# A new order of gate products and cache work, with GpSimd's page work given to VectorE and ScalarE

## The reference, cut to what matters

```
h = rms_norm(x) ; z = h @ w_in                  # u (512) | q | k | v (1024 each) | two gates (1024 each)
gate_pool = sigmoid(z[gates 0:1024]) ; gate_attn = sigmoid(z[gates 1024:])
pool_out  = _pool_mixer(u) ; o = attention(q, k, v)       # samples: over 512 cached positions + their own
merged = gate_pool * (pool_out @ w_pool_proj) + gate_attn * (o @ w_attn_proj)
x = x + merged @ w_o ; x = x + relu(rms_norm(x) @ w_up)^2 @ w_down ; y = rms_norm(x)

s = einsum('bqhcd,bkhcd->bhcqk', q, k) * HEAD_DIM ** -0.5  # two maps c per head
p = softmax(s) ; a = p[:, :, 0] - lam * p[:, :, 1] ; out = einsum('bhqk,bkhe->bqhe', a, v)
```

## Time and profile before

| | us |
|---|---|
| three runs, median | 1803.35 |
| the profiled execution | 1804.24 |
| its span (first to last instruction) | 1802.4 |
| TensorE busy | 1725.0 |
| VectorE busy | 1057.7 |
| ScalarE busy | 632.8 |
| GpSimd busy | 247.4 |
| DMA | 139.13 MB, mean 77 GB/s |

### The profile page before, as it was taken

How to read it: one execution, slowest core, us unless ns; L and a number is a source line. 1 busy time by engine, 2 the same in 40 slices (tenths; PEclk the granted TensorE clock), 3 DMA queues, 4 the chain that set the end, 5 groups by cost and what they waited for, 6 DMA issues and landing times.

```text
span 1802.4 us, 29113 instructions
## 1 busy us (share of the span) xinstructions
PE 1725.0 (96%) x11756; PEld 1668.6 (93%) x11756; DVE 1057.7 (59%) x1725; ACT 632.8 (35%) x1289; POOL 247.4 (14%) x284
## 2 busy tenths in 40 slices
PE   7999999999978788999999999999999999999997
PEld 6889888988958788999999999999999999999997
DVE  5677777777765986774223448454636363636454
ACT  4355555555543211113112445232414141414232
POOL 3222221222210655340000000000000000000001
PEclk9999999999979899999999999999999999999999
DMA  6202220221122565663112321211111111202112
GB/s 192 63 10 62 71 59 13 72 60 32 52 65 81 202 225 175 195 200 98 47 47 71 94 59 48 71 32 63 48 47 48 48 47 48 69 26 71 35 49 95
DMA packets 136525, 139.13 MB, mean 77 GB/s; under 512 B 6720, under 2 KB 114176, under 8 KB 136383
## 3 DMA queue, kind: packets, MB, share of 16 engines
q1 hardware_dynamic: 135239, 133.07, 23.8%
q10 hardware_dynamic: 1152, 4.19, 0.6%
HBM read 120.29 MB, written 17.18 MB: 76 GB/s over the span
## 4 chain that ended last, share of the span: by engine, by line
PE 83%; DVE 6%; POOL 3%; DMA 2%; issue 2%; ACT 2%; SPq 1%; DVEq 0%; ACTq 0%
PE ps L1072 20%; PE ps L782 18%; PE ps L1010 18%; PE ps L692 15%; PE ps L716 3%; PE ps L749 3%; POOL kv_pages L2138 2%; PE ps L739 1%; DMA q_bc<-q_sample_scratch 1%; POOL kv_pages L2144 1%; DVE kv_pages L1796 1%; DMA kv_pages<-in_cache_v 1%; DVE w_lo L1467 1%; PE ps L720 1%; DMA w_raw<-in_w_in 1%
## 5 line engine op out<-in xcount | busy, mean ns | idle before, releaser
L1988 DVE TENSOR_TENSOR x<-ps,x 128x1032 f32<-128x1032 f32 x64 | 78.9, 1232 | 223.4 <-PE ps L1072 223.4
L692 PE MATMUL ps<-w_hi,h_hi 128*128 128x384 f32 x520 | 182.3, 351 | 5.9 <-DVE w_lo L1467 3.8
L692 PE MATMUL ps<-w_hi,h_lo 128*128 128x384 f32 x520 | 176.7, 340 | 0.0
L692 PE MATMUL ps<-w_lo,h_hi 128*128 128x384 f32 x520 | 176.1, 339 | 0.0
L1072 PE MATMUL ps<-ff_lo,m_hi 128*128 128x344 f32 x768 | 162.9, 321 | 0.0
L1072 PE MATMUL ps<-ff_hi,m_lo 128*128 128x344 f32 x768 | 162.4, 320 | 0.0
L1072 PE MATMUL ps<-ff_hi,m_hi 128*128 128x344 f32 x768 | 162.1, 319 | 0.0
L1072 PEld LDWEIGHTS ps<-ff_lo,m_hi 128*128 128x128 f32 x768 | 129.1, 188 | 0.0
L1072 PEld LDWEIGHTS ps<-ff_hi,m_hi 128*128 128x128 f32 x768 | 128.4, 188 | 0.0
L1072 PEld LDWEIGHTS ps<-ff_hi,m_lo 128*128 128x128 f32 x768 | 128.2, 188 | 0.0
L1135 ACT ACTIVATE prob<-ps,nbias 128x256 f32<-128x256 f32 (+7 forms) x128 | 94.9, 742 | 88.9 <-DVE nbias L1526 86.4
(11 more groups left out here) (273 smaller groups left out, 4131.5 us busy)
## 6 DMA issues: line engine op xcount, KB each, us to landing
w_raw<-in_w_in SPq DMA_DIRECT2D x44, 512.0 KB, 6.0
kv_pages<-in_cache_k SPq DMA_DIRECT2D x32, 512.0 KB, 5.0
kv_pages<-in_cache_v SPq DMA_DIRECT2D x32, 512.0 KB, 5.1
m_pair<-in_w_up SPq DMA_DIRECT2D x16, 1024.0 KB, 5.5
m_down<-in_w_down SPq DMA_DIRECT2D x16, 1024.0 KB, 5.0
out<-kv_st SPq DMA_DIRECT2D x16, 512.0 KB
x_in<-in_x_prompt SPq DMA_DIRECT2D x8, 512.0 KB, 5.1
attention_out_scratch<-oT_st ACTq DMA_DIRECT2D x8, 512.0 KB, 2.6
```

Of the source, the lines that this page charges most:

```text
L692: mm = pe.matmul(bank[0:n, 0:3 * P], a[:, kt, toks(t)], w[:, :, kt, :], start=(kt == 0 and m == 0), stop=(kt == KT - 1 and m == 2))
L1988: dve.tensor_tensor(x1_chunks[:, n], psum_set(n % 2), x1_chunks[:, n], ALU.add).then_inc(s_xadd, 1)
```

## The change: what it does

The two hand-written loops go away: `PART_A` now holds all tiles up to the last `ga`, and the eight `ap` tiles follow in a row. Gates 6 and 7 move to the front, between the u tiles, and write to `merged[6]` and `merged[7]` themselves, since `gate` is one tile; `ga` results go to a new `ga_sig` of eight tiles. `up`, `o_hi` and `mg_lo` get other places: `o_hi` lies where `h_lo` was, so each of its tiles waits until the last `ga` product has read that k-tile (`s_hread`).

VectorE multiplies all four key pages in one instruction. Of the value pages VectorE still weighs two, and ScalarE the other two, in 16 instructions of 128x128 with a scale column. GpSimd does no page work. The work on the value pages moves from beside gate and pool tiles 4 to 7 to the last three pool tiles and the `ga` tiles. SP's order is written from step numbers: `V_LOAD_AT` says ahead of which weight load the value pages go.

The diff, cut to its core:

```diff
-PART_A = [("u", 0), ("u", 1), ("grp", 0), ("u", 2), ("grp", 1), ("u", 3), ("grp", 2), ("gate", 0), ("grp", 3),
-          ("pool", 0), ("gate", 1), ("pool", 1), ("gate", 2), ("pool", 2),
-          ("gate", 3), ("pool", 3)]
-REDUCE_AT = (1, 3, 5, 7, 9, 10, 11, 13)
+PART_A = [("u", 0), ("u", 1), ("gate", 6), ("grp", 0), ("u", 2), ("gate", 7), ("grp", 1), ("u", 3), ("grp", 2),
+          ("gate", 0), ("grp", 3), ("pool", 0), ("gate", 1), ("pool", 1), ("gate", 2), ("pool", 2), ("gate", 3), ("pool", 3),
+          ("gate", 4), ("pool", 4), ("gate", 5), ("pool", 5), ("pool", 6), ("pool", 7)] + [("ga", n) for n in range(KT)]
+OWN_AT, SCORES_AT, SELECT_AT, TAIL_AT = 5, 20, 21, 10
+REDUCE_AT = (2, 6, 10, 12, 13, 15, 16, 18)
+VALUES_AT = (23, 24, 25, 26, 27, 27, 28, 29)
+V_LOAD_AT = REDUCE_AT[6:] + (23, 23, 24, 25, 26, 27)
...
 # SP
+            def load_values(b):
+                if b < 2:
+                    sp.wait_ge(s_kred, DEC - 1 + b)
+                else:
+                    sp.wait_ge(s_v, b - 1)
+                load_pages(b, b % 2, cache_v)
...
+            for l in range(4, len(tile_at) + KT):
+                freed = (tile_at + list(range(S_ATTN, S_OUT)))[l - 4]
+                for b in range(2, DEC):
+                    if before <= REDUCE_AT[b - 2] < freed:
+                        load_keys(b)
+                for b in range(DEC):
+                    if before <= V_LOAD_AT[b] < freed:
+                        load_values(b)
+                if before <= TAIL_AT < freed:
+                    store_tail()
+                if before <= SELECT_AT < freed:
+                    load_samples()
...
+                if l < len(tile_at):
+                    load_a(l)
+                else:
+                    load(l // 2, l % 2, w_attn, KT, l - len(tile_at))
+                before = freed
...
 # TensorE: value sums b after these k-tiles
+            beside = {("u", 1): {1: last_head_out, 3: state_transposes}, ("ga", 0): {5: values_of(1)},
+                      ("ga", 1): {5: values_of(2)}, ("ga", 2): {1: values_of(3)}, ("ga", 3): {1: values_of(4), 7: values_of(5)},
+                      ("ga", 4): {5: values_of(6)}, ("ga", 5): {5: values_of(7)},
+                      ("ga", 6): {0: sample_norms, 3: spread_norms}}
...
+                if s_ == VALUES_AT[0]:
+                    cached_values(0)
...
 # ScalarE
+            def weigh_half(b):
+
+                act.wait_ge(s_pg[b % 2], PG_K + 16 * PAGES * (b // 2 + 1))
+                for g in range(PAGES // 2, PAGES):
+                    for h in range(HEADS):
+                        part = kv_pg[:, b % 2, g, h * P:(h + 1) * P]
+                        done = act.activation(part, part, ACT.Copy, scale=a_all[:, g, b * HEADS + h:b * HEADS + h + 1])
+                done.then_inc(s_vp, 1)
...
+                elif kind == "ga":
+                    if n == KT - 1:
+                        attention_high()
+                    sigmoid(t, chunks(ga_sig[:, n]))
+                    next_high(t)
+                    if n == 0:
+                        weigh_half(3)
+                    elif n == 1:
+                        weigh_half(4)
+                        weigh_half(5)
+                    elif n == 2:
+                        weigh_half(6)
+                    elif n == 3:
+                        weigh_half(7)
...
+                    if n == KT - 2:
+                        weigh_half(1)
+                    elif n == KT - 1:
+                        weigh_half(2)
...
 # VectorE
-                dve.tensor_tensor(kv_pg[:, b % 2, PAGES - 1], kv_pg[:, b % 2, PAGES - 1], q_bc[b % 2][:],
-                                  ALU.mult).then_inc(s_prod2, 1)
+                dve.tensor_tensor(kv_pg[:, b % 2], kv_pg[:, b % 2], q_bc[b % 2][:].unsqueeze(1).to_broadcast([P, PAGES, D]),
+                                  ALU.mult).then_inc(s_prod, 1)
...
+                elif kind == "ga":
+                    if n == 0:
+                        weigh_values(3)
+                        sum_values(2)
+                    elif n == 1:
+                        sum_values(3)
+                        weigh_values(4)
+                    elif n == 2:
+                        weigh_values(5)
+                        sum_values(4)
+                    elif n == 3:
+                        sum_values(5)
+                        weigh_values(6)
+                    elif n == 4:
+                        weigh_values(7)
+                        sum_values(6)
+                        sum_values(7)
+                    elif n == KT - 3:
+                        sample_outputs()
+                    elif n == KT - 2:
+                        sample_rows()
+                    elif n == KT - 1:
+                        attention_low()
+                    next_low(t)
...
+                    if n == N_EARLY - 1:
+                        weigh_values(0)
+                        weigh_values(1)
+                    elif n == KT - 2:
+                        sum_values(0)
+                    elif n == KT - 1:
+                        sum_values(1)
+                        weigh_values(2)
...
 # GpSimd
-            for b in range(DEC):
-                pool.wait_ge(s_pg[b % 2], 80 * (b // 2) + 80)
-                for g in range(PAGES - 1):
-                    part = kv_pg[:, b % 2, g]
-                    pool.tensor_tensor(part, part, q_bc[b % 2][:], ALU.mult).then_inc(s_prod, 1)
-            pool.wait_ge(s_vout, 1)
-            for i in range(0, DEC // 2):
-                for slot in range(2):
-                    pool.wait_ge(s_pg[slot], PG_K + 16 * PAGES * (i + 1))
-                    for g in range(PAGES // 2, PAGES):
-                        pool.tensor_tensor(*weighing(2 * i + slot, slot, g, 1), ALU.mult).then_inc(s_vp, 1)
```

More of the change, by code:

```diff
@@ L586, in _ @@
             load_keys(1)
[L587 to L599, removed]
@@ L614, in _, with store_tail @@
[L614 to L623, removed]
+            def store_tail():
+                sp.wait_ge(s_tailc, 1)
+                sp.dma_start(new_pool_p[0, 0], tail_st[0:BUF]).then_inc(s_out, 16)
+                sp.dma_start(new_pool_s[0, :, BUF - 1], tail_st[BUF:BUF + DEC]).then_inc(s_out, 16)
@@ L910, in select_weights, with cached_values, last_rows_ready @@
                 pe.matmul(bank_o[:, 256:320], ones_a[:], sel[:], start=True, stop=True).then_inc(s_sela, 1)
-            def cached_values(i, slot):
-                pe.wait_ge(s_vs, VS * (2 * i + slot + 1))
+            def cached_values(b):
+                pe.wait_ge(s_vout, 2)
+                pe.wait_ge(s_vs, VS * (b + 1))
                 for h in range(HEADS):
-                    mm = pe.matmul(ps[:, 6, bass.ds((2 * i + slot) * HEADS + h, 1)], kv_pg[:, slot, 0, h * P:(h + 1) * P],
+                    mm = pe.matmul(ps[:, 6, b * HEADS + h:b * HEADS + h + 1], kv_pg[:, b % 2, 0, h * P:(h + 1) * P],
                                    ones[:, 0:1], start=True, stop=True)
                 mm.then_inc(s_v, 1)
[L920 to L940, removed]
-            for i in range(0, DEC // 2):
[L942 to L945, removed]
-            for i in range(DEC // 2, KT - N_A):
-                product(gate_tile(i), h_hi, h_lo, KT)
-                product(pool_tile(i), y_hi, y_lo, NG)
+            def last_rows_ready():
+                tile_out(pe, at["grp", NG - 1])
             n_bh = DEC * HEADS
@@ L1734, in sample_softmax, with weigh_values, sum_values @@
                 dve.tensor_scalar(ones_a[:], ones[:], dst[:, 10:11], None, ALU.mult).then_inc(s_soft, 1)
+            def weigh_values(b):
+                if b == 0:
+                    dve.wait_ge(s_vout, 1)
+                dve.wait_ge(s_pg[b % 2], PG_K + 16 * PAGES * (b // 2 + 1))
+                dve.tensor_tensor(*weighing(b, b % 2, 0), ALU.mult).then_inc(s_vw, 1)
+            def sum_values(b):
+                slot = b % 2
+                dve.wait_ge(s_vp, b + 1)
+                dve.wait_ge(s_vw, b + 1)
+                dve.tensor_tensor(kv_pg[:, slot, 0:2], kv_pg[:, slot, 0:2], kv_pg[:, slot, 2:4], ALU.add).then_inc(s_vs, 1)
+                dve.wait_ge(s_vs, VS * b + 1)
+                dve.tensor_tensor(kv_pg[:, slot, 0], kv_pg[:, slot, 0], kv_pg[:, slot, 1], ALU.add).then_inc(s_vs, 1)
@@ L1736, in _, with attention_low @@
+            def attention_low():
+                for h in range(HEADS):
+                    dve.wait_ge(s_ohi, h + 1)
+                    dve.tensor_tensor(o_lo[:, h], o_raw[:, h], o_hi[:, h].bitcast(F32), ALU.subtract).then_inc(s_olo, 1)
             dve.wait_ge(s_ust, 1)
@@ L1831, in _ @@
-            for h in range(HEADS):
-                dve.wait_ge(s_ohi, h + 1)
-                dve.tensor_tensor(o_lo[:, h], o_raw[:, h], o_hi[:, h].bitcast(F32), ALU.subtract).then_inc(s_olo, 1)
             def attention_tile(n):
```

274 lines of the change are left out of this document (126 added, 148 removed).

## The result

The changed kernel takes 1806.78 us, the median of 20 runs (1803.11 to 1810.58), against 1803.76 for the kernel before in 20 runs beside it (1798.88 to 1807.97): ratio 1.0018, 95% interval [1.001, 1.0027]. It is 3.0 us slower, real by the interval but just short of the 0.2% I had named. The forecast was 1809.3 in a range of 1796 to 1819. The profiled execution takes 1806.34 us (span 1804.3).

A forecast was written before the change was run, and what follows sets the result against it. TensorE was taken to bound the kernel, with 39 us of losses between the second u product and last projection. After, 7.7 + 37.9 = 45.6 (+6.6; schedule +5.6), taken as +6: 1809.3 against median 1803.35, range 1796 to 1819.

The forecast's parts named there:

- the chain: Value pages behind the ga products: loads, weighing, additions and value sums wait on each other; 90.6 us, TensorE losing 35.5.
- the stretch that the forecast was about: Second u product to last attention projection, 567.63 to 988.16 us before; predicted to end at 993.8, +5.6.
- c(1): TensorE's value sum 1 (the number is the value's); its end is time 0 of the predicted value-page schedule.
- 30 or more as the sign: Three growing TensorE waits for value page sums in the ga products, 30 us or more together, would confirm the forecast.
- The holes of 5, 13 and 15 us: TensorE's three predicted holes among the ga products, from late value sums; low clock after the last adds 2.4 us.
- my schedule: Start-to-end layout with the margins, ending the attention projections at 993.8 us instead of 988.16, +5.6.
- ScalarE's half: ScalarE weighing two pages of each value in 16 pieces of 128x128: 5.2 us, bounds 3.3 and 6.7.
- Part one: The u, gate and pool products: pl_lo waits go, smaller waits and low clock leave 7.7 us of losses, bounds 3 and 16.
- 1.5 each: Low-clock cost behind two of the longer waits in the u, gate and pool products, 3 us together.
- The rival by which VectorE falls behind in the keys: Disturbed 7.1 us key multiplies make pooling late, costing TensorE 1.5 to 2 us per row: 1818; chance 0.09 (beyond 1819).
- quicker links: Same value-page dependencies, but page loads of 9.7 without sharing and ScalarE pieces at 0.20 take 8 off: about 1801; chance 0.23.
- SP's queue does not bind: Weight loads never hold value-page loads, only slot reuse does: losses 28, 1792; chance 0.13, shared with other ways to be faster.

The follow-up runs named there:

- e1: Changed kernel with SP issuing value pages 5 and 7 ahead of the weight load they stood behind; 1797.31 us, ratio 0.9967 against the kernel before.
- e2: Changed kernel with VectorE summing values 2, 4 and 6 before weighing pages 3, 5 and 7; 1785.55 us, ratio 0.9894 against the kernel before.
- e3: Changed kernel with both order edits, SP's of e1 and VectorE's of e2; 1779.91 us, ratio 0.9873 against the kernel before.
- e7: e3 plus SP issuing value pages 6 and 7 earlier and VectorE summing value 6 right after weighing it; 1770.86 us, ratio 0.9813.
- e8: e7 with GpSimd multiplying three of four key pages again; 1767.27 us, ratio 0.9793 against the kernel before.
- e5: Changed kernel with GpSimd multiplying three of four key pages again, all orders kept; 1804.22 us, ratio 0.9994 against the kernel before.
- e4: Changed kernel with GpSimd instead of ScalarE weighing the second two pages of each value; 1822.58 us, ratio 1.0104 against the kernel before.
- e6: Kernel before, with VectorE multiplying all four key pages and GpSimd out of the keys, order kept; 1803.51 us, ratio 0.9995.

## Why the prediction was right, and where its sizes were off

The mechanism was right at both ends, and the time lies in the range, but that it came as near as half of the forecast's +6 is in part luck: two errors in the chain cancelled, and the stretch that the forecast was about grew by only 0.5 us in the profiles. The order of gates removed the `pl_lo` waits, and the value pages became one chain, in which SP's page loads wait for a `w_lo` and that for the weighing. The steps, counted from the end of c(1) (764.45 us in the profile after):

```
                     predicted   measured
pages 3 landed          10.1        9.6
c(2) starts, ends    16.1, 18.1   15.5, 19.0
pages 4 landed          28.7       28.4
pages 5 landed          43.4       42.4
c(4) starts, ends    49.4, 51.4   48.3, 51.8
w_lo, weight load       71.4       69.6
pages 7 landed          82.6       79.8
c(6) starts, ends    88.6, 90.6   85.7, 89.2
```

- **The chain.** 89.2 us against 90.6. TensorE has 55.1 us of work in it, so it loses 34.1, where the prediction said 35.5. But only 25.6 us of it is idle time; I had named 30 or more as the sign. The other 8.5 is half clock, in the three late value sums (5.1) and in the products behind c(2) and c(4). The holes of 5, 13 and 15 us that I named did not fit my own times either: less the k-tiles and the value sum in between (11.4 us, then 19 twice), these give 4.7, 12.3 and 18.2, low clock included. e1 and e2 show the two causes one by one. The ends of the projections (of one profile each) and the medians, both less those of the changed kernel:

```
                            projections end    median
e1  SP's order               977.24    -9.7      -9.5
e2  VectorE's order          971.80   -15.2     -21.2
e3  both                     961.87   -25.1     -26.9
e7  the chain opened         952.10   -34.9     -35.9
e8  e7, keys on GpSimd       951.32   -35.7     -39.5
e5  keys on GpSimd           986.87    -0.1      -2.6
e4  values' half on GpSimd  1005.17   +18.2     +15.8
```

- **Links.** Two errors met in the chain and cancelled; that was luck. Page loads take 9.4 to 9.8 us, not 10.1 or 10.6, and a `w_lo` to landed pages 10.2 to 10.5, not 11.2; why they are quicker no run shows. With my added 0.5 for sharing and a load of pages 6 that started at the release of its slot, the five loads took 5.3 us less than in my schedule, and ScalarE's half with what follows it 0.4. Against that, each value sum behind a wait takes 3.55 us, not 2.0, at the half clock; I had counted that clock only behind the last hole. That lengthens the chain by 1.55 us each, 4.6 in all, since the slot is released only at the end of the sum.
- **ScalarE's half.** 16 pieces take 4.8 us, mean 388 ns. The view of ScalarE's groups:

```profile
L1271 ACT ACTIVATE kv_pages<-kv_pages,a_all 128x128 f32<-128x128 f32 x128 | 38.3, 388 | 49.1 <-DMA kv_pages<-in_cache_v 49.1
```

  My 5.2 was built from a copy and another column; the Trainium skill, ScalarE: Activation LUTs, "What ACT_TABLE_LOAD costs", gave an estimated 4.8, and the trace agrees with the page.
- **Part one.** 7.7 us predicted, 4.8 measured. Here the term for the low clock, "1.5 each", was mis-sized: the granted clock of the whole window is 1.00. The waits came where I had put them: gate 6 1.35 (predicted 1.4), gate 3 1.70 (1.9), `y_lo` 0.5 (0.3), `ones_a` (made in the softmax) 0.9 (0.7), the first value sum 0.4 (0.4). The 3 us of low clock did not: behind the wait at gate 3, TensorE's timeline has the full-clock 0.64 us from the second group on.

```profile
686.48 0.74 PE L788 MATMUL ps<-h_hi,w_hi 128*128 128x344 f32 x3 [1.70 <-DVE w_lo L1678]
687.05 0.64 PE L788 MATMUL ps<-h_lo,w_hi 128*128 128x344 f32 x3
```

- **The key row.** 4.42 + 4.42 us, as predicted (VectorE's groups of the profile after):

```profile
L1740 DVE TENSOR_REDUCE sc_all<-kv_pages 128x64 f32<-128x4096 f32 x8 | 35.4, 4420 | 0.3
L1737 DVE TENSOR_TENSOR kv_pages<-kv_pages,q_bc 128x4096 f32<-128x4096 f32 x8 | 35.3, 4417 | 0.0
```

  The rival by which VectorE falls behind in the keys did not happen.
- **The sum.** My schedule ended the projections at 993.8, measured on the time axis of the kernel before. After, they end at 986.98, and that execution reached the second u product 1.67 us earlier (565.96 against 567.63). Set on the same axis the end is at 988.65, 5.1 below my schedule. Of this, 3.0 is the low clock that part one did not have and 1.4 came in the chain; the remaining 0.7 I can't place. So the stretch is 0.5 us longer, not 5.6. The earlier start may belong to the change: the eight profiles in the new order reach the second u product at 565.9 to 566.8 us, the two in the old order at 567.6 and 568.0. Why is open.
- **What stays open.** The medians differ by 3.0 us [1.8 to 4.9], and the stretch by 0.5 in one profile each. The spans differ by 1.9: -1.7 at the start, +0.5 here, and some 3 in one place that was not changed. At 1095 us, behind the same 2.6 us wait of TensorE for `part_p` (a partial sum that ScalarE copies out), the clock stays low for longer (windows, before and then after):

```profile
1095.00:1105.00 10.00, 10.00 (x76) 9.96 (x76) 7.22 (x12) 5.83 (x9) 2.55 (x2) 0.86 0.00 0
```

```profile
1095.00:1105.00 10.00, 10.00 (x53) 9.96 (x52) 6.17 (x11) 4.02 (x6) 2.55 (x2) 0.54 0.00 0
```

  53 matmuls instead of 76 in 10 us. Over 1040 to 1160 us the clock is 0.99 in the kernel before, e1, e4, e6 and e8, and 0.96 or 0.97 in the changed kernel, e2, e3, e5 and e7. The time from the end of the projections to the end of the span follows it: 813.6 to 814.3 us in the first group, 815.8 to 817.6 in the second. Kernels in the new order stand on both sides, the two in the old order on one; whether the change makes the spell more frequent can't be told from one profile a kernel. Without it, the stretch alone says "no change". So the cause of the measured 3.0 us as a whole is not shown; what is shown is that two effects of over 30 us each nearly cancel in the stretch.

The rivals: quicker links (1801) was right about the links. Loads and ScalarE's half together gave 5.7 of the 8 us that it asked for; the half clock in the value sums, which neither it nor my forecast had, took 4.6 back. "SP's queue does not bind" (1792) is refuted by e1, which has to change the order to gain 9.5 us.

**Who should do the work.** For the keys it hardly matters: GpSimd's share is worth nothing in the old order (e6), and in the new one the medians favour it by 2.6 us (e5, where the intervals just touch) and 3.6 us (e8), of which the stretch up to the last projection shows 0.1 and 0.5. The value pages' half is better on ScalarE, by 15.8 us (e4), some 8 of them in the chain.

## What to carry to other kernels

When a slot's reload stands in an in-order queue, ask for each issue in front of it what that one waits for: here a weight load waiting for another engine's `w_lo` held page loads whose slot was free, and VectorE's "weigh the next, then sum this one" held a sum whose data was there. Put what needs only a free slot ahead of what needs a computed value, and finish one item before starting on the next where the consumer waits for the first. A change that moves the time by 3 us may hold two effects of over 30 us each; the windows by stage show them, the total does not. Here three moved calls and one tuple turned +0.2% into -1.9%.

## What the runs showed of the hardware that I had not expected

- A value sum of 16 one-column matmuls that follows a wait of 3.96 us or more takes 3.54 or 3.55 us, at a granted clock of 0.50 throughout; once, in e5 behind 4.12 us, it took 3.25, at 0.55. Behind no wait or one of 0.38 us it takes 1.84 to 1.92.
- A wait of 1.35 or 1.70 us ahead of wide matmuls left the clock at 1.00 (window 565.96 to 752.20), but in the kernel before 1.73 us ahead of a value sum was followed by 0.62 from 750 to 754 us. Even the same wait does not always end alike: behind 0.38 us ahead of c(0) and the value sum itself, the clock stayed at 1.00 in the changed kernel and e7, and was 0.65 for some 4.9 us in e5 and e8, which cost 1.5 us.
- The same wait of 2.61 us for `part_p` was followed by 10 us at a clock of 0.86 in one profile and 0.54 in another.
- What GpSimd disturbs depends on where the overlap falls: in the earlier trace rows the weighing took 3.98 us, in e4 the weighing of pages 3 took its plain 2.29, and the additions behind it 3.98 and 2.80; a `w_lo` beside GpSimd's half of pages 5 took 2.92 instead of 1.22.
